# A hybrid decoder layer on one core: the high halves of two weight sets are kept in DRAM as well

## The chip, the cores and the metric

One core of one Trainium2 chip runs the kernel. The metric is the device time of one execution in microseconds; lower is better.

## The reference, cut to what is computed

One decoder layer is applied to 2048 prompt tokens and to 8 x 8 sample tokens, all in float32:

```python
h = rmsnorm(x, g_pre_mix)
z, q, k, v, glow, og = jnp.split(h @ w_in, SPLIT_IDX, axis=-1)          # 1024 -> 2064
pool_out = pool_mixer(z, ...)          # causal windows 2, 4, 8, 16, then a 128x128 map per group
gla_out = gla_mixer(q, k, v, gk, og)   # gated linear attention, 4 heads, exact per token
x = x + rmsnorm(concat(pool_out, gla_out) @ w_o, g_post_mix)
f = conv_ffn(rmsnorm(x, g_pre_ffn), ..., w_up, w_conv, b_conv, w_down)  # d_ff 2816, gated
x = x + rmsnorm(f, g_post_ffn)
x = x + (p @ w_ple) * jax.nn.sigmoid(x @ w_ple_gate)
```

## The kernel before

The tokens are cut into six tiles, `TILES`: tile 0 has 256 prompt tokens and the 64 sample tokens, tiles 1 to 4 have 384 prompt tokens each, tile 5 has 256. Features lie on the partitions and tokens in the columns. Every product with a large weight is made of three, since each operand is split into a high half, rounded to the matmul's float32r form, and a low half, the rest: high x high, high x low (weight), low (activation) x high. They are lines L1640, L1641 and L1642 in the function `product`.

The weights don't fit on the chip, so they stream past it once a tile. They are cut into *units* of 128 output columns, 512 KB each, in the fixed order that `plan` writes out: 16 units `in` (w_in), 8 units `o` (w_o), 44 units `up`, 24 parts `down`, 2 halves of `ple` and 8 units `gate`. In the text in5 means unit 5 of `in` of the tile at hand, gate3 unit 3 of `gate`. The ple halves and the gates of tile t are computed inside tile t+1: after in15 come the first ple half and gate0 to gate2, then o0 to o7, then the second ple half and gate3 to gate7, then up0. So tile 0's gates run in tile 1. Those of tile 5 stand at the end of the kernel.

A unit n uses slot n % 4 of the four slots. A slot has two buffers of 4 KB a partition: `stage` (the same bytes as `w_lo`) and `w_hi` (the same bytes as `w_whole`). There are two ways through a slot. In the plain way SP loads the unit into `stage`, ACT rounds it into `w_hi` (L730), and DVE subtracts in place, so that `w_lo` holds the low half (L1157). For `in` and `gate`, the low half that was made in the first pass is also stored to a DRAM tensor, `kept_lo` (L470). In all later passes SP loads the whole weights into `w_whole` (L483) and the low half into `w_lo` (L484), and ACT rounds in place; DVE has nothing to do.

The queues are in order and each engine's program follows the list of units. SP's is `load_unit(n)`: it first issues the stores of low halves that are due, up to unit n-3 (`keep_los(n - SLOTS + 1)`, each after a wait for `lo_made`), then waits until PE has ended unit n-4, waits for the landing of unit n-4's store if there was one, and then issues the load of unit n. All DMAs of the kernel are issued by SP on one queue. ACT, while PE is in unit n, first empties the bank of unit n-1 (`finish`), then makes the high half of unit n+2 (`make_hi(n + 2)`, which waits for its landing), and then does the rest of the work that is listed for this unit: decays, copies of v, squares, ple banks, copies of y. DVE makes the low half of unit n+1 (`make_lo(n + 1)`) ahead of its other work. PE waits for `hi_made` or `lo_made` at the start of a unit (`halves_ready`). The outputs go round over three PSUM banks, so PE also needs the bank of three outputs before.

Of the kernel before, what the change touches and what calls it, by code (L numbers as in the profile page):

```python
# [7 lines left out]
F32 = mybir.dt.float32  # L8
# [5 lines left out]
P = 128  # L14
D = 1024
KD = D // P
# [28 lines left out]
SLOTS = 4  # L45
# [17 lines left out]
def plan():  # L63

    units, outs, ticks = [], [], []

    def ple(t, s):
        units.append((t, "ple", s))
        for m in range(4 * s, 4 * s + 4):
            outs.append((t, "ple", m))  # L70
            ticks.append((t, "ple", m))

    def full(t, kind, m):
        for table in (units, outs, ticks):
            table.append((t, kind, m))

    for t in range(NT):
        for s in range(16):
            full(t, "in", s)
            if s >= 8 and s - 8 < chunks(t) + (TILES[t][2] > 0):  # L80
                outs.append((t, "v", s - 8))
        if t:
            ple(t - 1, 0)
            for m in range(EARLY_GATES):
                full(t - 1, "gate", m)
        for m in range(KD):
            full(t, "o", m)
        if t:
            ple(t - 1, 1)
            for m in range(EARLY_GATES, KD):  # L90
                full(t - 1, "gate", m)
        for m in range(2 * NF):
            full(t, "up", m)
        for m in range(3 * KD):
            units.append((t, "down", m))
            ticks.append((t, "down", m))
            if m % 3 == 0:
                outs.append((t, "down", m // 3))
    for s in range(2):
        ple(LAST, s)  # L100
    for m in range(KD):
        full(LAST, "gate", m)
    return units, outs, ticks


UNITS, OUTS, TICKS = plan()

KEPT_NO = {unit[1:]: j for j, unit in enumerate(unit for unit in UNITS if unit[0] == 0 and unit[1] in ("in", "gate"))}
KEEP_LO = [unit[0] == 0 and unit[1:] in KEPT_NO for unit in UNITS]
LOADS_LO = [unit[0] > 0 and unit[1:] in KEPT_NO for unit in UNITS]  # L110
LOS_MADE = list(itertools.accumulate(not loaded for loaded in LOADS_LO))
UNIT_NO = {name: n for n, name in enumerate(UNITS)}
OUT_NO = {name: n for n, name in enumerate(OUTS)}
# [33 lines left out]

def hybrid_layer(nc, x_prompt, x_sample, state_pool, state_gla, state_conv, p_prompt, p_sample, packed,
                 w_in_units, w_o_units, w_up_units, w_down_units, w_ple_units, w_gate_units,
                 kept_lo, y_prompt, y_sample, pool_prompt, gla_prompt, conv_prompt, pool_sample, gla_sample,  # L150
                 conv_sample):
    ctx = ExitStack()
    with ctx:
# [10 lines left out]
        def at(name, shape, offset, dtype=F32):  # L164
            return nc.alloc_sbuf_tensor_at(name, shape, dtype, offset=offset)
# [50 lines left out]
        w_lo = [at(f"w_lo{s}", [P, KD, P], slot_at[s], F32R) for s in range(SLOTS)]  # L216
        hi_at = [region(KD * P) for _ in range(SLOTS)]
        w_hi = [at(f"w_hi{s}", [P, KD, P], hi_at[s], F32R) for s in range(SLOTS)]
        w_whole = [at(f"w_whole{s}", [P, KD, P], hi_at[s]) for s in range(SLOTS)]
# [96 lines left out]
        def sem(name):  # L316
            return ctx.enter_context(nc.semaphore(name))
# [7 lines left out]
        landed = [sem(f"landed{s}") for s in range(SLOTS)]  # L325
        kept = [sem(f"kept{s}") for s in range(SLOTS)]
        hi_made, lo_made, ticks = sem("hi_made"), sem("lo_made"), sem("ticks")
# [72 lines left out]
        def exact(ap):  # L400
            return ap.bitcast(F32)
# [31 lines left out]
        def landing(n):  # L433

            return landed[n % SLOTS], 16 * sum(1 + LOADS_LO[k] for k in range(n % SLOTS, n + 1, SLOTS))

        def keeping(n):
            return kept[n % SLOTS], 16 * sum(KEEP_LO[k] for k in range(n % SLOTS, n + 1, SLOTS))

        def tick(name):  # L440
            return ticks, TICK_NO[name] + 1
# [1 line left out]
        def end_tick(unit):  # L443
            t, kind, m = unit
            return tick((t, "ple", 4 * m + 3)) if kind == "ple" else tick(unit)

        def parts_of(unit):
            return DOWN_PARTS[unit[2] % 3][1] if unit[1] == "down" else KD
# [3 lines left out]

        @block.sync
        def _(sp):
            keep_next = [0]

            def source(unit):
                t, kind, m = unit
                if kind == "down":
                    first_k, parts = DOWN_PARTS[m % 3]  # L460
                    return w_down_units[m // 3, :, first_k:first_k + parts, :]
                return {"in": w_in_units, "o": w_o_units, "up": w_up_units, "ple": w_ple_units,
                        "gate": w_gate_units}[kind][m]


            def keep_los(n):
                for k in range(keep_next[0], n + 1):
                    if KEEP_LO[k]:
                        sp.wait_ge(lo_made, LOS_MADE[k])
                        sp.dma_start(kept_lo[KEPT_NO[UNITS[k][1:]]], exact(w_lo[k % SLOTS][:, :, :])).then_inc(  # L470
                            kept[k % SLOTS], 16)
                keep_next[0] = n + 1

            def load_unit(n):
                unit = UNITS[n]
                if n >= SLOTS:
                    keep_los(n - SLOTS + 1)
                    sp.wait_ge(*end_tick(UNITS[n - SLOTS]))
                    if KEEP_LO[n - SLOTS]:
                        sp.wait_ge(*keeping(n - SLOTS))  # L480
                if LOADS_LO[n]:
                    s = n % SLOTS
                    sp.dma_start(w_whole[s][:, :, :], source(unit)).then_inc(landed[s], 16)  # L483
                    sp.dma_start(exact(w_lo[s][:, :, :]), kept_lo[KEPT_NO[unit[1:]]]).then_inc(landed[s], 16)  # L484
                    return
                dst = stage[n % SLOTS][:, 0:parts_of(unit), :]
                if unit[1] == "ple":
                    dst = dst.rearrange("p (k c) d -> p k (c d)", k=2)
                sp.dma_start(dst, source(unit)).then_inc(landed[n % SLOTS], 16)
# [36 lines left out]

            load_first_x()
            load_unit(0)
            sp.dma_start(const[:, 0:C_GK], packed[:, 0:C_GK]).then_inc(const_loaded, 16)
            load_unit(1)  # L530
            sp.dma_start(const[:, C_GK:C_ALL], packed[:, C_GK:C_ALL]).then_inc(tables_loaded, 16)
            load_unit(2)
            zs = state_pool[0].rearrange("b t (g c) -> (b t g) c", g=POOLG).rearrange("(q p) c -> p q c", p=120)
            sp.dma_start(z_state_tok[:, :, :], zs).then_inc(states_loaded, 16)
# [8 lines left out]
            for n in range(SLOTS, len(UNITS)):  # L543
                t, kind, m = UNITS[n]
# [170 lines left out]
        def _(act):  # L715
# [4 lines left out]
            def make_hi(n):  # L720
                for k in range(hi_next[0], min(n + 1, len(UNITS))):
                    one_hi(k)
                hi_next[0] = max(hi_next[0], n + 1)

            def one_hi(n):
                if n < len(UNITS):
                    s, parts = n % SLOTS, parts_of(UNITS[n])
                    whole = w_whole[s] if LOADS_LO[n] else stage[s]
                    act.wait_ge(*landing(n))
                    act.activation(w_hi[s][:, 0:parts, :], whole[:, 0:parts, :], ACT.Copy).then_inc(hi_made, 1)  # L730
# [408 lines left out]
        def _(dve):  # L1139
# [8 lines left out]
            def make_lo(n):  # L1148
                for k in range(lo_next[0], min(n + 1, len(UNITS))):
                    one_lo(k)  # L1150
                lo_next[0] = max(lo_next[0], n + 1)

            def one_lo(n):
                if n < len(UNITS) and not LOADS_LO[n]:
                    s, parts = n % SLOTS, parts_of(UNITS[n])
                    dve.wait_ge(hi_made, n + 1)
                    dve.tensor_tensor(w_lo[s][:, 0:parts, :], stage[s][:, 0:parts, :], exact(w_hi[s][:, 0:parts, :]),  # L1157
                                      ALU.subtract).then_inc(lo_made, 1)

# [463 lines left out]
        def _(pe):  # L1623
# [261 lines left out]
                y_turned.did(last, t, m)  # L1885

            def halves_ready(n):
                if LOADS_LO[n]:
                    pe.wait_ge(hi_made, n + 1)
                else:  # L1890
                    pe.wait_ge(lo_made, LOS_MADE[n])

# [250 lines left out]
```

## Time and profile before

| | |
|---|---|
| median of 3 runs | 2621.26 us (2618.65 to 2623.07) |
| the profiled execution | 2621.26 us, span 2619.6 us |
| PE busy | 2572.4 us (98%), mean granted clock 0.993 |
| DVE, ACT busy | 1578.4 us (60%), 1355.1 us (52%) |
| DMA | 415.95 MB, mean 159 GB/s; written to DRAM 22.89 MB |
| chain that ended last | PE 94%, DVE 2%, ACT 2%, DMA 1% |

The span is what the trace covers, from the first instruction to the last. In the rows further down a unit is a run of 24 products on PE. In SP's timeline a line is the issue of a DMA, not its transfer: how long a transfer takes is its time from issue to landing. A wait stands in square brackets behind the instruction that waited, with its length and what ended it.

### The profile page before, as it was taken

To read this page: it belongs to the slowest core of one execution; us is meant where nothing else is said; L and a number is where in the kernel's file an instruction comes from. 1 tells how busy PE (TensorE), PEld (TensorE's weight loads), DVE (VectorE), ACT (ScalarE), POOL (GpSimd) and SP (SyncE) were. 2 spreads that over 40 slices of the span, in tenths; PEclk is the share of its full clock that TensorE was granted. 3 is DMA by queue.
4 is the path that set the end of the run, shared out by engine and by line. 5 is a ranking of instruction groups with operands and counts; after the bars stand their busy time and mean duration, and the time that the engine had idled before them with its cause. 6 is when DMAs were issued, how large, how long until landed. Compare 5 with 4: busy or idle time off the path is not lost.

```text
span 2619.6 us, 41342 instructions
## 1 busy us (share of the span) xinstructions
PE 2572.4 (98%) x16538; PEld 2508.1 (96%) x16538; DVE 1578.4 (60%) x2525; ACT 1355.1 (52%) x2156; POOL 163.7 (6%) x492
## 2 busy tenths in 40 slices
PE   7989999999999999999999999999999999999998
PEld 6889999999999999999999999999999999999997
DVE  5668754566665455666545666554556654547864
ACT  4555554555444456544445654444565444566554
POOL 3200100100000010000001000000100000100000
PEclk9999999999999999999999999999999999999999
DMA  7435546454434644443464444345444434755565
GB/s 205 145 101 177 161 142 211 148 165 143 147 124 125 207 139 165 148 151 121 123 207 143 163 145 153 124 118 206 145 161 146 144 125 124 263 178 193 187 180 196
DMA packets 123107, 415.95 MB, mean 159 GB/s; under 512 B 12862, under 2 KB 21222, under 8 KB 122918
## 3 DMA queue, kind: packets, MB, share of 16 engines
q1 hardware_dynamic: 122918, 413.32, 48.2%
q8 instruction: 132, 2.16, 0.3%
q14 instruction: 57, 0.47, 0.1%
HBM read 390.38 MB, written 22.89 MB: 158 GB/s over the span
## 4 chain that ended last, share of the span: by engine, by line
PE 94%; DVE 2%; ACT 2%; DMA 1%; issue 1%; SPq 0%; DVEq 0%; ACTq 0%
PE G L1640 29%; PE G L1641 28%; PE G L1642 28%; PE X L1699 2%; PE X L1633 1%; PE X L1636 1%; DMA w_lo<-kept_lo 1%; PE X L1826 1%; PE X L1754 1%; PE X L1769 0%; ACT w_hi L730 0%; DVE w_lo L1157 0%; PE G L1633 0%; DVE A L1248 0%; PE X L1678 0%
## 5 line engine op out<-in xcount | busy, mean ns | idle before, releaser
L1640 PE MATMUL G<-h_hi,w_hi 128*128 128x384 f32 (+2 forms) x3264 | 1070.6, 328 | 16.9 <-DVE w_lo L1157 6.8
L1641 PE MATMUL G<-h_hi,w_lo 128*128 128x384 f32 (+2 forms) x3264 | 1052.3, 322 | 0.0
L1642 PE MATMUL G<-h_lo,w_hi 128*128 128x384 f32 (+2 forms) x3264 | 1052.3, 322 | 0.0
L730 ACT ACTIVATE w_hi<-stage 128x1024 fp32r<-128x1024 f32 (+1 forms) x492 | 510.6, 1038 | 397.2 <-DMA stage<-in_w_up_units_dram 236.0
L1157 DVE TENSOR_TENSOR w_lo<-stage,w_hi 128x1024 fp32r<-128x1024 f32 (+1 forms) x492 | 588.1, 1196 | 161.6 <-ACT w_hi L730 161.3
L1640 PEld LDWEIGHTS G<-h_hi,w_hi 128*128 128x128 f32 x3264 | 617.9, 189 | 23.4 <-issue 10.3
L1641 PEld LDWEIGHTS G<-h_hi,w_lo 128*128 128x128 f32 x3264 | 618.4, 189 | 1.7 <-issue 0.4
L1642 PEld LDWEIGHTS G<-h_lo,w_hi 128*128 128x128 f32 x3264 | 617.6, 189 | 0.0
L1640 PE MATMUL G<-y_hi,w_hi 128*128 128x384 f32 (+2 forms) x1056 | 346.3, 328 | 0.0
L1642 PE MATMUL G<-y_lo,w_hi 128*128 128x384 f32 (+2 forms) x1056 | 339.6, 322 | 0.0
L1641 PE MATMUL G<-y_hi,w_lo 128*128 128x384 f32 (+2 forms) x1056 | 339.5, 321 | 0.0
L1420 DVE SCALAR_TENSOR_TENSOR cg<-gx,const,cg 128x384 f32<-128x384 f32 (+1 forms) x264 | 151.5, 574 | 85.8 <-ACT cg L902 62.2
L1640 PEld LDWEIGHTS G<-y_hi,w_hi 128*128 128x128 f32 x1056 | 199.0, 188 | 4.0 <-issue 2.9
L1641 PEld LDWEIGHTS G<-y_hi,w_lo 128*128 128x128 f32 x1056 | 199.1, 189 | 1.1
L1642 PEld LDWEIGHTS G<-y_lo,w_hi 128*128 128x128 f32 x1056 | 198.9, 188 | 0.0
L1408 DVE TENSOR_TENSOR gx<-G,rms_up 128x384 f32<-128x384 f32 (+1 forms) x132 | 67.5, 511 | 197.8 <-PE G L1642 179.5
L730 ACT ACTIVATE w_hi<-w_whole 128x1024 fp32r<-128x1024 f32 x120 | 126.7, 1056 | 67.0 <-DMA w_lo<-kept_lo 66.4
L1165 DVE TENSOR_TENSOR total<-total,sq 128x384 f32<-128x384 f32 (+2 forms) x119 | 62.4, 524 | 157.2 <-ACT sq L743 156.9
L909 ACT ACTIVATE cg<-cg 128x384 f32<-128x384 f32 (+2 forms) x132 | 65.9, 500 | 173.7 <-DVE cg L1420 141.5
L1640 PE MATMUL G<-xg_hi,w_hi 128*128 128x384 f32 (+2 forms) x384 | 128.3, 334 | 3.8 <-DVE xg_lo L1459 2.3
L743 ACT ACTIVATE sq<-G 128x384 f32<-128x384 f32 (+2 forms) x84 | 39.1, 465 | 167.7 <-PE G L1642 167.7
L1642 PE MATMUL G<-xg_lo,w_hi 128*128 128x384 f32 (+2 forms) x384 | 123.4, 321 | 0.0
(234 smaller groups left out, 2673.9 us busy)
## 6 DMA issues: line engine op xcount, KB each, us to landing
stage<-in_w_up_units_dram SPq DMA_DIRECT2D x264, 512.0 KB, 3.5
w_lo<-kept_lo SPq DMA_DIRECT2D x120, 512.0 KB, 4.5
stage<-in_w_down_units_dram SPq DMA_DIRECT2D x96, 448.0 KB, 3.3
w_whole<-in_w_in_units_dram SPq DMA_DIRECT2D x80, 512.0 KB, 3.5
stage<-in_w_o_units_dram SPq DMA_DIRECT2D x48, 512.0 KB, 3.5
stage<-in_w_down_units_dram SPq DMA_DIRECT2D x48, 512.0 KB, 3.5
w_whole<-in_w_gate_units_dram SPq DMA_DIRECT2D x40, 512.0 KB, 3.6
kept_lo<-w_lo SPq DMA_DIRECT2D x24, 512.0 KB, 5.2
```

Of the source, the lines that this page charges most:

```text
L730: act.activation(w_hi[s][:, 0:parts, :], whole[:, 0:parts, :], ACT.Copy).then_inc(hi_made, 1)
L743: squared.did(act.activation(out[:, 0:width(t)], src[:, 0:width(t)], ACT.Square), t, m)
L909: gelu_made.did(act.activation(c[:, 0:w], c[:, 0:w], ACT.Gelu_apprx_tanh), t, f)
L1157: dve.tensor_tensor(w_lo[s][:, 0:parts, :], stage[s][:, 0:parts, :], exact(w_hi[s][:, 0:parts, :]), ALU.subtract).then_inc(lo_made, 1)
L1165: added.did(dve.tensor_tensor(start[:, 0:w], start[:, 0:w], ring[:, m % 2, 0:w], ALU.add), t, m - 1)
L1408: last = dve.tensor_tensor(x[:, 2:2 + np_], G[b][:, 0:np_], rms_up[:, 0:np_], ALU.mult)
L1420: last = dve.scalar_tensor_tensor(c[:, 0:np_], x[:, k:k + np_], tap, c[:, 0:np_], ALU.mult, ALU.add)
L1633: return pe.transpose(out, in_, ident[0:n, 0:n])
L1640: pe.matmul(ps[:, 0:w], l_hi, r_hi[:, 0:w], start=start, stop=False)
L1641: pe.matmul(ps[:, 0:w], l_lo, r_hi[:, 0:w], start=False, stop=False)
L1642: return pe.matmul(ps[:, 0:w], l_hi, r_lo[:, 0:w], start=False, stop=stop)
L1699: last = pe.matmul(X[first + b][:, col:col + 64], opnd[n % 2][r, d, cols(c)], queries[n % 2][r, d, 64 * c:64 * c + 64], start=True, stop=True)
```

## The change

The high halves of `in` and `gate` are kept in DRAM too. A new tensor `kept_hi` takes them. For `gate` both halves are stored in the first pass (tile 0's gates). For `in` the low half is stored in the first pass, as before, and the high half in the second (tile 1), in which it is still made by ACT from the whole weights. After that (`in` from tile 2 on, `gate` from tile 1's gates on) SP loads the high half straight into `w_hi`, ACT makes nothing for these units, and PE waits for the landing itself. The stores are issued at another place: `keep_halves(n - SLOTS)` is called directly ahead of the load of unit n, for the unit whose slot that load will overwrite, where the stores up to unit n-3 were issued before. SP's wait for the landing of the stores stays where it was, behind the wait for PE's end of unit n-4, and now also covers the high half's.

```diff
+KEEP_HI = [unit[1:] in KEPT_NO and unit[0] == (1 if unit[1] == "in" else 0) for unit in UNITS]
 LOADS_LO = [unit[0] > 0 and unit[1:] in KEPT_NO for unit in UNITS]
+LOADS_HI = [lo and not hi for lo, hi in zip(LOADS_LO, KEEP_HI)]
+HIS_MADE = list(itertools.accumulate(not loaded for loaded in LOADS_HI))
...
         def keeping(n):
-            return kept[n % SLOTS], 16 * sum(KEEP_LO[k] for k in range(n % SLOTS, n + 1, SLOTS))
+            return kept[n % SLOTS], 16 * sum(KEEP_LO[k] + KEEP_HI[k] for k in range(n % SLOTS, n + 1, SLOTS))
...
-            def keep_los(n):
-                for k in range(keep_next[0], n + 1):
-                    if KEEP_LO[k]:
-                        sp.wait_ge(lo_made, LOS_MADE[k])
-                        sp.dma_start(kept_lo[KEPT_NO[UNITS[k][1:]]], exact(w_lo[k % SLOTS][:, :, :])).then_inc(
-                            kept[k % SLOTS], 16)
-                keep_next[0] = n + 1
+            def keep_halves(n):
+                s, name = n % SLOTS, UNITS[n][1:]
+                if KEEP_HI[n]:
+                    sp.wait_ge(hi_made, HIS_MADE[n])
+                    sp.dma_start(kept_hi[KEPT_NO[name]], exact(w_hi[s][:, :, :])).then_inc(kept[s], 16)
+                if KEEP_LO[n]:
+                    sp.wait_ge(lo_made, LOS_MADE[n])
+                    sp.dma_start(kept_lo[KEPT_NO[name]], exact(w_lo[s][:, :, :])).then_inc(kept[s], 16)
 
             def load_unit(n):
                 unit = UNITS[n]
                 if n >= SLOTS:
-                    keep_los(n - SLOTS + 1)
+                    keep_halves(n - SLOTS)
                     sp.wait_ge(*end_tick(UNITS[n - SLOTS]))
-                    if KEEP_LO[n - SLOTS]:
+                    if KEEP_LO[n - SLOTS] or KEEP_HI[n - SLOTS]:
                         sp.wait_ge(*keeping(n - SLOTS))
                 if LOADS_LO[n]:
-                    s = n % SLOTS
-                    sp.dma_start(w_whole[s][:, :, :], source(unit)).then_inc(landed[s], 16)
-                    sp.dma_start(exact(w_lo[s][:, :, :]), kept_lo[KEPT_NO[unit[1:]]]).then_inc(landed[s], 16)
+                    s, j = n % SLOTS, KEPT_NO[unit[1:]]
+                    if LOADS_HI[n]:
+                        sp.dma_start(exact(w_hi[s][:, :, :]), kept_hi[j]).then_inc(landed[s], 16)
+                    else:
+                        sp.dma_start(w_whole[s][:, :, :], source(unit)).then_inc(landed[s], 16)
+                    sp.dma_start(exact(w_lo[s][:, :, :]), kept_lo[j]).then_inc(landed[s], 16)
                     return
...
             def one_hi(n):
-                if n < len(UNITS):
+                if n < len(UNITS) and not LOADS_HI[n]:
...
             def halves_ready(n):
-                if LOADS_LO[n]:
-                    pe.wait_ge(hi_made, n + 1)
+                if LOADS_HI[n]:
+                    pe.wait_ge(*landing(n))
+                elif LOADS_LO[n]:
+                    pe.wait_ge(hi_made, HIS_MADE[n])
                 else:
                     pe.wait_ge(lo_made, LOS_MADE[n])
```

## Rows read from the trace of the kernel before

**Rows 1.** The page, parts 1 and 4: busy time and last chain, by engine.

```profile
PE 2572.4 (98%) x16538; PEld 2508.1 (96%) x16538; DVE 1578.4 (60%) x2525; ACT 1355.1 (52%) x2156; POOL 163.7 (6%) x492
...
PE 94%; DVE 2%; ACT 2%; DMA 1%; issue 1%; SPq 0%; DVEq 0%; ACTq 0%
```

**Rows 2.** The page, part 5: the splitting of the weights on DVE and ACT.

```profile
L1157 DVE TENSOR_TENSOR w_lo<-stage,w_hi 128x1024 fp32r<-128x1024 f32 (+1 forms) x492 | 588.1, 1196 | 161.6 <-ACT w_hi L730 161.3
...
L730 ACT ACTIVATE w_hi<-w_whole 128x1024 fp32r<-128x1024 f32 x120 | 126.7, 1056 | 67.0 <-DMA w_lo<-kept_lo 66.4
```

**Rows 3.** The page, part 6: DMA issues, median us from issue to landing.

```profile
w_lo<-kept_lo SPq DMA_DIRECT2D x120, 512.0 KB, 4.5
...
w_whole<-in_w_in_units_dram SPq DMA_DIRECT2D x80, 512.0 KB, 3.5
...
kept_lo<-w_lo SPq DMA_DIRECT2D x24, 512.0 KB, 5.2
```

**Rows 4.** The DMA queue's timeline in tile 0 (start, length, what).

```profile
41.81 0.38 SPq L489 DMA_DIRECT2D stage<-in_w_in_units_dram  x1
...
83.26 0.33 SPq L489 DMA_DIRECT2D stage<-in_w_in_units_dram  x1
83.64 0.43 SPq L470 DMA_DIRECT2D kept_lo<-w_lo  x1
...
103.66 5.58 SPq L489 DMA_DIRECT2D stage<-in_w_o_units_dram  x2
```

**Rows 5.** The DMA queue's timeline in tile 1: the loads of in3 and in13.

```profile
413.74 0.33 SPq L483 DMA_DIRECT2D w_whole<-in_w_in_units_dram  x1
...
468.16 0.33 SPq L483 DMA_DIRECT2D w_whole<-in_w_in_units_dram  x1
```

**Rows 6.** DMA issues at 77.9, 572.5, 1130.5 and 1130.9, 1131.8: us to landing.

```profile
kept_lo<-w_lo SPq DMA_DIRECT2D x1, 512.0 KB, 5.4
...
kept_lo<-w_lo SPq DMA_DIRECT2D x1, 512.0 KB, 2.9
...
stage<-in_w_up_units_dram SPq DMA_DIRECT2D x1, 512.0 KB, 4.0
x_tok<-in_x_prompt_dram SPq DMA_DIRECT2D x1, 512.0 KB, 4.8
...
x_tok<-in_x_prompt_dram SPq DMA_DIRECT2D x1, 512.0 KB, 6.7
```

**Rows 7.** ACT's timeline in tile 1, at the first half of ple.

```profile
504.44 1.05 ACT L730 ACTIVATE w_hi<-stage 128x1024 fp32r<-128x1024 f32 x1
```

**Rows 8.** PE's timeline there: the start of ple, and a wait.

```profile
505.50 0.39 PE L1640 MATMUL G<-p_hi,w_hi 128*128 128x320 f32 x1
...
509.36 0.42 PE L1640 MATMUL G<-p_hi,w_hi 128*128 128x320 f32 x1 [0.98 <-ACT ple L949]
```

**Rows 9.** The DMA queue's timeline in tile 1: the load of gate6.

```profile
564.72 0.33 SPq L489 DMA_DIRECT2D stage<-in_w_gate_units_dram  x1
```

**Rows 10.** PE's timeline in tile 1: the first product of up3.

```profile
602.17 0.33 PE L1640 MATMUL G<-h_hi,w_hi 128*128 128x384 f32 x1
```

**Rows 11.** Windows on PE: busy us by engine, granted clock, DMA share, GB/s.

```profile
160.00:166.00 6.00, 4.22 (x14) 3.86 (x15) 5.86 (x14) 3.61 (x9) 0.00 (x0) 0.59 0.00 0
...
2575.00:2581.00 6.00, 4.21 (x22) 3.83 (x21) 0.51 (x2) 3.73 (x8) 0.00 (x0) 0.72 0.69 226
```

**Rows 12.** The waits of PE in tiles 2 to 4 (total us, times, longest).

```profile
PE G L1640 <- ACT ple L949: 3.7, 4, 2.1
```

**Rows 13.** ACT's and PE's timelines in the last 45 us.

```profile
2575.89 1.06 ACT L730 ACTIVATE w_hi<-w_whole 128x1024 fp32r<-128x1024 f32 x1 [1.87 <-DMA w_lo<-kept_lo]
...
2590.26 1.04 ACT L730 ACTIVATE w_hi<-w_whole 128x1024 fp32r<-128x1024 f32 x1
...
2577.27 0.39 PE L1640 MATMUL G<-p_hi,w_hi 128*128 128x256 f32 x1 [1.79 <-ACT ple_last L949]
...
2604.52 0.44 PE L1633 MATMUL X<-ident,sig 128*128 128x128 f32 x2 [1.00 <-ACT y_tok L965]
```

More of the change, by code:

```diff
@@ L149, in hybrid_layer @@
                  w_in_units, w_o_units, w_up_units, w_down_units, w_ple_units, w_gate_units,
-                 kept_lo, y_prompt, y_sample, pool_prompt, gla_prompt, conv_prompt, pool_sample, gla_sample,
+                 kept_hi, kept_lo, y_prompt, y_sample, pool_prompt, gla_prompt, conv_prompt, pool_sample, gla_sample,
                  conv_sample):
@@ L454, in _ @@
         def _(sp):
-            keep_next = [0]
             def source(unit):
@@ L1155, in one_lo @@
                     s, parts = n % SLOTS, parts_of(UNITS[n])
-                    dve.wait_ge(hi_made, n + 1)
+                    dve.wait_ge(hi_made, HIS_MADE[n])
                     dve.tensor_tensor(w_lo[s][:, 0:parts, :], stage[s][:, 0:parts, :], exact(w_hi[s][:, 0:parts, :]),
@@ L2136 @@
         args.append(nc.dram_tensor(f"in_{name}_dram", a.shape, F32, kind="ExternalInput").ap())
-    args.append(nc.dram_tensor("kept_lo", (len(KEPT_NO), P, KD, P), F32, kind="Internal").ap())
+    for name in ("kept_hi", "kept_lo"):
+        args.append(nc.dram_tensor(name, (len(KEPT_NO), P, KD, P), F32, kind="Internal").ap())
     for n, shape in enumerate(_OUTS):
```

## The prediction

> **What bounds the kernel now.** I read the page first. PE is busy for 98% of the span, and 94% of the chain that ended last is PE's [rows 1], so the kernel can gain at most the 47 us in which PE idles, and anything that makes PE wait is paid in full. The splitting of weights costs ACT 1.06 us and DVE 1.2 us a unit [rows 2], but both engines have room: ACT is busy 52%, DVE 60% [rows 1]. The question is therefore which PE waits end on the work that is removed, and which new ones end on the work that is added. So I read next the waits of PE, then the timeline of the DMA queue, which shows when each unit's slot is refilled, then the landings, and last ACT's timeline where it holds PE up.
>
> **What the DMA queue does today.** SP issues the load of unit n when PE has ended unit n-4, so the issue times are also PE's pace. The load has three units of time before PE needs it. A store of a low half is issued one unit before the slot is wanted again: it goes out at 83.64, right behind the load of 83.26 [rows 4], and the wait for it comes only one load later. That is why 24 stores of 5.2 us each [rows 3] cost nothing.
>
> **Part 1: the stores move onto the queue's own path.** In the new code the store of unit n-4 is issued immediately ahead of load n, and SP then waits for it to land before load n goes out. It thus sits behind load n-1, which went out a moment before, and queued behind SP's wait are load n and all that follow. One load and the landing of one store must now pass in each step. I call this the round trip.
>
> In tile 0 (in1 to in15) a step is one load and one store. The store is issued 0.38 us after the load [rows 4] and lands 5.4 us later [rows 6]: P0 = 5.8 us. PE's pace there is (103.66 - 41.81)/12 = 5.15 us a unit [rows 4]. SP loses 0.65 us a unit, some 8 to 9 us by the last one. A unit's slack is three units less landing and splits, 15.5 - 7 = 8.5 us. So this uses up the slack and costs PE about 1 us; the bounds are 0 and 5 (5.8 against 6.2 us a step).
>
> **Part 2: 24 stores more.** The high halves of tile 1's in units, and of tile 0's gates (computed in tile 1), are stored too.
>
> *Tile 1, in units.* A step is now two loads and one store. The second load is issued some 0.4 us after the first (the first's issue takes 0.33 [rows 5]) and lands 4.5 us later [rows 3]: both are there after 4.9 us. No row shows three. Below: four loads in a row were issued from 1130.5 to 1131.8; the first lands at 1134.5, the second at 1135.7, the fourth at 1138.5 [rows 6], so one more transfer of 512 KB adds 1.2 to 1.4 us at the queue's full rate: with 1.25, 6.15 us. Above: a store behind a load adds 5.8 - 3.5 = 2.3 us [rows 3, 6]: 7.2 us. I take the middle, P1 = 6.7. PE's pace is (505.5 - 413.74)/16 = 5.7 us a unit [rows 5, 8], less than even the low end. The step repeats 13 times from the load of in3 at 413.74 to the load of the first ple half, then twice with one load and one store (P0) to the load of gate1: 413.74 + 13 x 6.7 + 2 x 5.8 = 512.4. It needs 4.0 us to land (the first of the four loads) [rows 6] and 1.05 us of ACT [rows 7]: 517.5. ACT does this work at PE's start of ple, ahead of everything that follows there, and PE's start is 505.5 [rows 8]. So PE is 12.0 us late by then. With P1 = 6.15 it is 4.9, with 7.2 it is 18.5. Part of it shows earlier, in the in units: ACT waits in order for the landing of the unit two ahead, and the decays, the copies of v and so the PSUM banks stand behind that wait; in10 starts at 468.16 today [rows 5], and in11's load would go out at 413.74 + 8 x 6.7 = 467.3. These are the same 12 us, not more.
>
> *Tile 1, gates 3 to 7.* A step is one load and two stores: 5.8 + 1.25 = 7.1 us, or at most 5.8 + 2.3 = 8.1. There are five, from the load of gate6 at 564.72 [rows 9] to that of up3: 600.2. Landing 3.5 [rows 3], 1.06 and 1.2 for the halves [rows 2] make 606.0, and PE starts up3 at 602.17 [rows 10]: 3.8 us late. I take 5, since the subtraction also stands in order among DVE's other work. With 8.1 it is 9. Gates 0 to 2 have the same step three times ahead of o units, and the 12 us of lateness covers them.
>
> *The clock.* Where PE had idled 3.7 us the granted clock in the next 6 us was 0.59, and 0.72 around a wait of 1.8 us [rows 11]; the level falls from 2.4 GHz to 1.2 for a part of them. New waits of this kind cost some 2 us more (0 to 4), as the queue catches up in the meantime.
>
> The Trainium skill (DMA: Bandwidth & Descriptors, on the two cost components of a DMA) puts the fixed cost of a DMA mostly on the confirmation of the write and calls a target in HBM the heaviest. The trace has a lone store at 2.9 us and a lone load at 3.5 [rows 3, 6], which disagrees, but 0.9 us more for a store than for a load behind a load, which agrees; by the rule alone P1 would be the upper bound. The same page fits 2.0 us plus bytes over 436 GB/s; an estimate from it for 1.5 MB is 5.6 us, less than PE's pace, and the new waits would vanish.
>
> **Part 3: what ACT is spared.** From tile 2 on (in units) and for the gates of tiles 1 to 5, 104 splits of 1.06 us vanish. Most lie beside PE's work and give nothing. Two places count. At the first ple half, ACT splits gate1 [rows 7] before it empties the ple banks, for which PE waits 0.98 us [rows 8]; tiles 2 to 4 show the same, 3.7 us in four waits [rows 12]. Four tiles (2 to 5) at 0.95: 4 us. At the end of the kernel, ACT waits 1.87 us for a gate's landing and splits it, and PE waits 1.79 us for the bank behind it; another split of 1.04 stands ahead of the first sigmoid, and a turn of y waits 1.00 us behind a third [rows 13]; with half a microsecond of slow clock [rows 11] that is 4 us. Together 8 us; 4 if the chain through DVE takes over at the end, 9 at most. That the high half now comes from the stored copy changes no bytes: two loads of 512 KB as before.
>
> **Sum.** +1 +12 +5 +2 -8 = +12 us on the profiled execution's 2621.26 us (span 2619.6 and 1.7 around it), which is also the median: 2633. Lower ends: 0 + 4.9 + 3.8 + 0 - 8 = +1, 2622. Upper ends: 5 + 18.5 + 9 + 4 - 4 = +32, 2653.
>
> **The rivals.**
> *The queue is quick enough* (other side). If two loads and a store pass in 5.7 us or less, because stores run beside loads on the 16 DMA engines, SP never falls behind in tile 1, and the gates' two stores stay inside the slack. Then the gain stands alone: 2621.3 - 8 = 2613. For it: the DMA engines are at 0.69 in a window with pairs of loads, not full [rows 11]. Against: a store behind a load is the slowest landing of all [rows 6]. It decides at a step of 5.7 us. The fit of the Trainium skill quoted above, 5.6, would put it here. Chance 0.15.
> *The costs cancel.* A step near 6.2 us, tile 0 hidden: +9 - 8, so 2621 to 2623. For it: the rate of four loads in a row [rows 6]. Chance 0.2.
> *The waits feed each other.* ACT waits in order, so a late landing also holds decays, evacuations and DVE's subtractions; in tile 0 PE falls behind as well, and the clock drops more often. Tile 0 gives 10 instead of 1, the clock 8 instead of 2, steps of 7.2: about +45, 2665. Against: three units of slack. Chance 0.1.
> *No change*, since ACT and DVE are off the path anyway: this needs the stores to be hidden as well and the end's waits not to shrink; it lies inside the second.
>
> **How the numbers follow.** My forecast of 2633 has 0.55 (its own range 2623 to 2653), the others 0.15, 0.2, 0.1. A difference under 0.2% (5.2 us) is about what a measurement cannot tell from none. Faster than 2616: 0.16; within: 0.2 and a little of the forecast's low end, 0.22; slower than 2626.5: 0.62. The range 2616 to 2653 leaves out the first and the last rival, with the tails.
>
> **What would show it.** Right: SP's waits for kept stores become the largest waits of its queue in tile 1; its loads of in4 to in15 go out about 6.7 us apart; PE idles between 440 and 530 and again at 590 to 615, some 17 us in all; ple waits from tile 2 on are gone and the end after 2570 is about 4 us shorter. Wrong: a spacing under 5.8 us, or PE's new waits in tile 0, would move the sum to the first or third rival.

## The result, and the profile after

The changed kernel takes 2646.05 us (median of 4 runs, 2643.8 to 2649.27) against 2619.95 for the kernel before: ratio 1.010, interval 1.0083 to 1.0118. It is slower by 26 us. The forecast had the sign, but with 12 us less than half of the size.

The page of the changed kernel: busy time by engine, the DMA totals, the chain that ended last, and three of its DMA issues.

```profile
PE 2579.2 (98%) x16538; PEld 2515.1 (95%) x16538; DVE 1576.4 (60%) x2525; ACT 1253.9 (47%) x2052; POOL 160.2 (6%) x492
...
HBM read 390.38 MB, written 35.48 MB: 161 GB/s over the span
...
PE 91%; DMA 4%; DVE 2%; ACT 1%; issue 1%; SPq 0%; POOL 0%; DVEq 0%; POOLq 0%; ACTq 0%
...
w_lo<-kept_lo SPq DMA_DIRECT2D x120, 512.0 KB, 4.6
w_hi<-kept_hi SPq DMA_DIRECT2D x104, 512.0 KB, 3.7
...
kept_lo<-w_lo SPq DMA_DIRECT2D x24, 512.0 KB, 5.4
kept_hi<-w_hi SPq DMA_DIRECT2D x24, 512.0 KB, 6.2
```

ACT has lost the 104 splits (101 us less than in [rows 1]), and as many bytes are read as before. The new thing is DMA in the chain that ended last: 4% against 1% [rows 1]. What the DMA queue waited for (total us, times, longest) names it, in the kernel before and then in the changed one:

```profile
SPq L480 <- DMA kept_lo<-w_lo: 13.1, 8, 5.7
```

```profile
SPq L483 <- DMA kept_lo<-w_lo: 124.1, 24, 6.5
SPq L483 <- DMA kept_hi<-w_hi: 94.2, 16, 7.6
```

SP waits 218 us for stores to land, where it waited 13. Its timeline in tile 1, from the load of in3 on, answers to [rows 5]:

```profile
417.37 0.33 SPq L489 DMA_DIRECT2D w_whole<-in_w_in_units_dram  x1
417.74 0.43 SPq L490 DMA_DIRECT2D w_lo<-kept_lo  x1
418.22 0.43 SPq L472 DMA_DIRECT2D kept_hi<-w_hi  x1
425.18 0.33 SPq L489 DMA_DIRECT2D w_whole<-in_w_in_units_dram  x1
...
432.54 0.33 SPq L489 DMA_DIRECT2D w_whole<-in_w_in_units_dram  x1
...
439.77 0.33 SPq L489 DMA_DIRECT2D w_whole<-in_w_in_units_dram  x1
```

Two loads, a store, and then nothing until the store has landed. The median spacing from in3 to in15 is 7.3 us, where PE needs 5.7. Three of the steps took 7.8 to 8.9 us, so that the mean of the thirteen steps to the load of the first ple half is 7.5. The chain that ended last, in tile 1 of the changed kernel between 440 and 540 us (start, length, what; the first pieces of a row of twelve of this kind, and the end):

```profile
440.62 6.39 DMA kept_hi<-w_hi
447.92 6.34 DMA kept_hi<-w_hi
455.18 6.92 DMA kept_hi<-w_hi
...
515.33 5.00 DMA kept_hi<-w_hi
520.78 5.27 DMA kept_hi<-w_hi
526.11 4.44 DMA stage<-in_w_gate_units_dram
533.64 1.48 ACT out_sq L862
```

For this stretch 76% of the chain is the landing of one store after another. It ends as foreseen: in the load of gate1, ACT's work at the first ple half, and PE.

Where PE's lateness arises is seen by setting the same product of both traces side by side. The table gives PE's start in microseconds.

| first product of | before | changed | late by |
|---|---|---|---|
| in0, tile 0 | 22.4 | 23.5 | 1.1 |
| in0, tile 1 | 413.5 | 417.2 | 3.6 |
| gate0 (in tile 1) | 513.9 | 541.6 | 27.6 |
| up4, tile 1 | 606.3 | 642.3 | 35.9 |
| first ple half at the end | 2573.2 | 2601.4 | 28.3 |
| span | 2619.6 | 2642.8 | 23.2 |

So the start is 1.1 us later, tile 0 costs 2.6 us, tile 1's in units and ple half 24.0, tile 1's last gates 8.3, and all that follows gives back 12.7.

### The profile page after: what moved, and what is told of

The parts are those of the page before. It is cut to its first block, busy times and chain, and to the rows that moved or that the text cites. A ratio compares the mean times of both kernels' runs of the same rounds, so it can differ in the third digit from the quotient of the medians.

```text
span 2642.8 us, 41278 instructions
## 1 busy us (share of the span) xinstructions
PE 2579.2 (98%) x16538; PEld 2515.1 (95%) x16538; DVE 1576.4 (60%) x2525; ACT 1253.9 (47%) x2052; POOL 160.2 (6%) x492
## 4 chain that ended last, share of the span: by engine, by line
PE 91%; DMA 4%; DVE 2%; ACT 1%; issue 1%; SPq 0%; POOL 0%; DVEq 0%; POOLq 0%; ACTq 0%
PE G L1646 28%; PE G L1647 28%; PE G L1648 28%; DMA kept_hi<-w_hi 3%; PE X L1705 2%; PE X L1639 1%; PE X L1642 1%; DMA kept_lo<-w_lo 1%; PE X L1832 1%; PE X L1775 1%; PE X L1760 0%; DVE w_lo L1163 0%; DMA stage<-in_w_up_units_dram 0%; DMA stage<-in_w_in_units_dram 0%; PE X L1781 0%
## 5 line engine op out<-in xcount | busy, mean ns | idle before, releaser
L1647 PE MATMUL G<-xg_hi,w_lo 128*128 128x384 f32 (+2 forms) x384 | 124.1, 323 | 0.0
```

Of the source, the lines that this page charges most:

```text
L1647: pe.matmul(ps[:, 0:w], l_lo, r_hi[:, 0:w], start=False, stop=False)
```

## The experiments

Each kernel is compared with the kernel before in runs on the same chip. All are built from the changed kernel unless the text says otherwise. Their table stands after the last of them.

**The stores back at their old place.** The stores go out where the kernel before issues them; everything else is as changed.

```diff
-                    keep_halves(n - SLOTS)
+                    while keep_next[0] <= n - SLOTS + 1:
+                        keep_halves(keep_next[0])
+                        keep_next[0] += 1
```

> The changed kernel, but each unit's stores are issued where the kernel before issues them, up to unit n-3 ahead of load n, so that a store is waited for only one load later; the same 48 stores, the same bytes. Theory A (the loss is the round trip of a load and a store's landing that now stands on the queue's own path): the steps of 7.3 us in tile 1 and 5.7 us in tile 0 vanish, the spacing of the loads of tile 1 follows PE again (about 5.7 us), and what is left is the gain, which the trace of the changed kernel shows as 12.7 us from tile 2 on: 2607 us, 2603 to 2612. Theory B (the 12.6 MB of stores more slow the loads themselves): most of the 24 us of tile 1's in units and the 8 us of its last gates stay: 2630 us or more.

Measured: 2609.07 us against 2619.85, ratio 0.9958 (0.9946 to 0.9971). All 48 stores and their bytes are still there, and tile 1's cost is gone. Theory B falls. The landings in tile 1 between 415 and 490 us show how much slower the transfers may become without cost:

```profile
kept_hi<-w_hi SPq DMA_DIRECT2D x14, 512.0 KB, 8.3
w_whole<-in_w_in_units_dram SPq DMA_DIRECT2D x13, 512.0 KB, 5.2
w_lo<-kept_lo SPq DMA_DIRECT2D x13, 512.0 KB, 7.4
```

The changed kernel has its transfers of tile 1 land sooner (between 425 and 510 us):

```profile
w_whole<-in_w_in_units_dram SPq DMA_DIRECT2D x12, 512.0 KB, 4.1
w_lo<-kept_lo SPq DMA_DIRECT2D x12, 512.0 KB, 5.6
kept_hi<-w_hi SPq DMA_DIRECT2D x12, 512.0 KB, 6.4
```

It is the slower kernel by 37 us all the same. What counts is not how long a transfer takes but what is held back until it has landed.

**The late place alone.** The kernel before, with `keep_los(n - SLOTS)` for `keep_los(n - SLOTS + 1)`.

> The kernel before with one argument changed: the store of a low half is issued ahead of the load that overwrites its slot, one unit later than before; no high half is kept. Theory A: tile 0's steps are 5.7 to 5.8 us as in the changed kernel, where PE was 3.9 us late at the start of tile 0's up1 (5.3 from its best point); the last gates of tile 1 have steps of 5.8 us and need 0 to 1 us: plus 4 to 6 us, 2625 us. Theory B: the number of bytes is that of the kernel before, so 2620 us.

Measured: 2625.49 against 2619.85, ratio 1.0024 (1.0014 to 1.0033). The place costs time without a byte more, 5.6 us, as theory A had it. The profiled execution is only 2.5 us longer than that of before; in it tile 0 costs 2.8 us and tile 1's last gates 0.2.

**High halves of in units alone.** `KEEP_HI` and `LOADS_HI` are true for `in` only.

> The changed kernel, but high halves are kept for the in units alone; the gates are split on ACT each time, as before. Theory A: tile 0 costs 4 us, tile 1's in units and first ple half 24, its last gates 0 to 1; the gain is nearly gone, since the ple waits and the end of the kernel hang on the splits of gates (12.7 us less some 11): plus 26, 2646 us, as slow as the changed kernel with two thirds of its stores. Theory B: two thirds of the stores' 32 us of tile 1, 21, without the gain: 2641.

Measured: 2652.27, ratio 1.0123 (1.0109 to 1.0136), 6 us above the 2646 of theory A and further still from theory B. Tile 1's in units cost 23.1 us, its last gates 0.1. The kernel is 6 us slower than the changed one, which has more stores: the in units bring the loss and none of the gain. This run's first product starts 4.0 us later than in the trace of before. The start is shifted by -0.1 to 4.2 us in these traces, by 3.2 us also where the stores are at their old place, so it is not taken for an effect of the edits.

**The gain alone.** The first experiment without the stores of high halves; the high buffer is filled from the kept low halves.

```diff
-                if KEEP_HI[n]:
-                    sp.wait_ge(hi_made, HIS_MADE[n])
-                    sp.dma_start(kept_hi[KEPT_NO[name]], exact(w_hi[s][:, :, :])).then_inc(kept[s], 16)
...
-                        sp.dma_start(exact(w_hi[s][:, :, :]), kept_hi[j]).then_inc(landed[s], 16)
+                        sp.dma_start(exact(w_hi[s][:, :, :]), kept_lo[j]).then_inc(landed[s], 16)
```

> Leaves out: no high half is stored, and from tile 2 on (gates: tile 1) the buffer of the high half is loaded with the kept low half instead, so the values of these products are not those of the reference; bytes loaded, waits and splits left out are those of the changed kernel, and the low halves' stores stand where they did before. Both theories: no loss, only the gain of the splits that ACT is spared, 12.7 us: 2607 us. My prediction had 8: 2612.

Measured: 2608.09 against 2619.85: 11.8 us, close to the 12.7 expected. With the first experiment's 10.8 it says that 24 stores more cost 1 us, if anything, when they go out early; the intervals of the two overlap.

**The step made smaller, larger, and of another kind.** Three kernels change only what stands late in tile 1's in units: half the store, the store twice, and a load in the store's stead. The first and the third leave out what they don't store: from tile 2 on their in units load the kept low half into the high buffer, so these products are not the reference's.

```diff
+                    parts = KD if UNITS[n][1] == "gate" else KD // 2
-                    sp.dma_start(kept_hi[KEPT_NO[name]], exact(w_hi[s][:, :, :])).then_inc(kept[s], 16)
+                    sp.dma_start(kept_hi[KEPT_NO[name], :, 0:parts, :], exact(w_hi[s][:, 0:parts, :])).then_inc(kept[s], 16)
...
-                        sp.dma_start(exact(w_hi[s][:, :, :]), kept_hi[j]).then_inc(landed[s], 16)
+                        sp.dma_start(exact(w_hi[s][:, :, :]), (kept_lo if unit[1] == "in" else kept_hi)[j]).then_inc(landed[s], 16)
```

> The changed kernel, but in tile 1 only half of each in unit's high half (256 KB) is stored, at the same place; leaves out the other half, and from tile 2 on the in units load the kept low half into the high buffer, so their products are not the reference's. Measured step in tile 1 with the whole store: 7.3 us. If a store behind two loads costs by its bytes at the queue's full rate (0.6 us for 256 KB) and the rest is fixed, the step is 6.7 us, tile 1's in units and ple cost 15 instead of 24 us, and the time is 2637 us. If the whole 2.3 us of a store are bytes, the step is 6.15 and the time 2628 us. If it is all fixed: 7.3 us and 2646.

Measured: 2628.59, ratio 1.0031 (1.0021 to 1.0041), step 6.2 us: the second of the three cases. In the next edit `kept_hi` has twice the size and `keeping` counts the second store too.

```diff
                     sp.dma_start(kept_hi[KEPT_NO[name]], exact(w_hi[s][:, :, :])).then_inc(kept[s], 16)
+                    if UNITS[n][1] == "in":
+                        sp.dma_start(kept_hi[KEPT_NO[name] + len(KEPT_NO)], exact(w_hi[s][:, :, :])).then_inc(kept[s], 16)
```

> The changed kernel, but in tile 1 each in unit's high half is stored twice, the second time to DRAM that nobody reads. Theory A: the step grows by 1.3 us (full rate) to 8.6 us, PE's lateness by 13 such steps, 17 us, since all slack is used up already: 2663 us. With 2.3 us a store: 9.6 us and 2676. A theory in which the loss is not the step on the queue's path gives no more than 3 us: 2649.

Measured: 2675.28, ratio 1.0209 (1.0195 to 1.0223), step 9.2 us, near the case of 2.3 us a store (2676). In the next edit `spare` is a buffer that nobody uses; the load of the high buffer is as in the first of the three.

```diff
-                    sp.dma_start(kept_hi[KEPT_NO[name]], exact(w_hi[s][:, :, :])).then_inc(kept[s], 16)
+                    if UNITS[n][1] == "in":
+                        sp.dma_start(spare[:, :, :], w_in_units[UNITS[n][2]]).then_inc(kept[s], 16)
+                    else:
+                        sp.dma_start(kept_hi[KEPT_NO[name]], exact(w_hi[s][:, :, :])).then_inc(kept[s], 16)
```

> The changed kernel, but in tile 1 the late store of each in unit's high half is replaced by a load of the same 512 KB from DRAM into an unused buffer, issued and waited for at the same place; leaves out the stores, and from tile 2 on the in units load the kept low half into the high buffer, so their products are not the reference's. If only the third transfer counts, the step stays 7.3 us and the time 2646. If it is the store's direction that costs the 0.9 us more (three loads in a row took 6.4 us from the first issue), the step is 6.4, tile 1's in units and ple cost 8 to 11 us instead of 24, and the time is 2632 us.

Measured: 2636.66, ratio 1.0063 (1.0048 to 1.0078), step 6.6 us, between its two cases. Median landings in the three, in tile 1's in units; each fence shows the late transfer of one kernel, first the half store, then the double one (both of its stores), then the load, with the two loads ahead of it:

```profile
kept_hi<-w_hi SPq DMA_DIRECT2D x15, 256.0 KB, 5.2
```

```profile
kept_hi<-w_hi SPq DMA_DIRECT2D x30, 512.0 KB, 6.9
```

```profile
spare<-in_w_in_units_dram SPq DMA_DIRECT2D x14, 512.0 KB, 5.7
w_whole<-in_w_in_units_dram SPq DMA_DIRECT2D x12, 512.0 KB, 3.4
w_lo<-kept_lo SPq DMA_DIRECT2D x12, 512.0 KB, 4.5
```

What follows: half a store less takes 1.1 us off the step, so by its bytes a store of 512 KB costs 2.2 to 2.3 us there. The step without any late transfer would be 4.9 [rows 3], so of the store's 2.4 us hardly anything seems to be a fixed part; the half store also has rows of half the length, which no run separates. A second store adds 1.9. A load at the same place adds 1.7, 0.7 us less than a store. And a store slows the loads that were issued before it: they land after 4.1 and 5.6 us in the changed kernel, after 3.4 and 4.5 with a load behind them. The cost in tile 1 follows the step: 5.2 us at 6.2, 13.2 at 6.6, 24.0 at 7.3, 50.6 at 9.2. From the changed kernel to the double store that is 26.6/1.9 = 14 us for each microsecond of step, from the half store 17, for thirteen steps.

**Gates alone, early.** The first experiment with `KEEP_HI` and `LOADS_HI` true for `gate` only.

> High halves kept for the gates alone (8 stores of high halves instead of 24), stores issued early as in the kernel before. Theory: the splits of in units lie beside PE's work and give nothing, those of the gates give all: 2608 us, the same as with both kept and stored early (2609). Rival: the in units' splits give their share (64 of 104): 2614.

Measured: 2609.18, ratio 0.9960 (0.9948 to 0.9973): the same as with both kept. The 64 splits of in units are worth nothing that the runs can tell; the 40 of gates are the gain.

**Gates alone, late.** The changed kernel with `KEEP_HI` and `LOADS_HI` true for `gate` only.

> The changed kernel with high halves kept for the gates alone, stores late as in the change. By the steps of the earlier runs: tile 0 costs 2.7 us (late lows), tile 1's in units nothing (their step is two loads and no store), its last gates 8, and the gain is 11: plus 0, 2620 us (2617 to 2623), that is, two thirds of the high halves' stores gone and all of the loss but 8 us of it. If the loss hung on all 48 stores alike, a third of the high ones would leave some 11 of the 24 us: 2631.

Measured: 2623.22 against 2620.92, ratio 1.0010 (1.0001 to 1.0020), within the expected 2617 to 2623 but for 0.2 us. Tile 1's in units cost nothing, its last gates 7.2.

**The late store on another queue.** The in units' high halves are stored from ACT's queue when PE starts the unit. SP waits for them where it did.

```diff
-                if KEEP_HI[n]:
+                if KEEP_HI[n] and name[0] == "gate":
                     sp.wait_ge(hi_made, HIS_MADE[n])
...
+                if KEEP_HI[n] and kind == "in":
+                    act.wait_ge(hi_made, HIS_MADE[n])
+                    act.dma_start(kept_hi[KEPT_NO[(kind, m)]], exact(w_hi[n % SLOTS][:, :, :])).then_inc(kept[n % SLOTS], 16)
                 make_hi(n + 2)
```

> The changed kernel, but the in units' high halves are stored from ACT's queue when PE starts the unit, as late as SP does it, and SP only waits for them where it did; same 48 stores, same bytes. If the loss is the order on SP's own queue (a store issued behind a late load, and the next load behind that store's landing, so that the lateness is never made good), the spacing follows PE again (5.9 us), tile 1's in units cost 0 to 4 us, and the time is 2646 - 24 + 2 = 2624 us (2619 to 2630). If it is only that a store issued in PE's unit n-4 has to land before load n, wherever it is issued from, the step stays at 7 us and the time over 2640.

Measured: 2623.62 against 2620.92, ratio 1.0012 (1.0003 to 1.0021). Tile 1's in units cost 0.0 us, its last gates 9.6. SP's waits, and the landings between 425 and 510 us:

```profile
SPq L483 <- DMA kept_hi<-w_hi: 64.9, 16, 7.1
```

```profile
kept_hi<-w_hi ACTq DMA_DIRECT2D x14, 512.0 KB, 5.2
w_lo<-kept_lo SPq DMA_DIRECT2D x12, 512.0 KB, 6.0
```

SP still waits for these stores, and the loads land late, but the store's issue hangs on PE and not on the load before, so that a late load makes the next store no later. The lateness does not add up: three steps between in5 and in10 took 7.9 to 8.0 us, the ones behind them 1.5 to 4.6. One thing more is different: the store lands after 5.2 us, against 6.4 in the changed kernel, and this run doesn't tell how much of the cure is that. The second queue makes the loads no faster: the low half lands after 6.0 us, against 5.6. The Trainium skill (DMA: Bandwidth & Descriptors, on issuing engines that are not separate DMA queues) says the queues share the same 16 engines; the later loads agree.

All runs: the step is the median spacing of the loads from in3 to in15 of tile 1. The costs are differences of PE's position between the products named in the table above, less those of the trace before. "After up4" is the change from up4 to the end of the span.

| kernel | median us | step | tile 0 | in and ple, tile 1 | last gates | after up4 |
|---|---|---|---|---|---|---|
| changed | 2646.05 | 7.3 | 2.6 | 24.0 | 8.3 | -12.7 |
| stores at the old place | 2609.07 | 5.9 | -1.7 | 0.0 | 0.0 | -12.5 |
| late place alone | 2625.49 | 5.9 | 2.8 | 0.0 | 0.2 | -1.4 |
| in alone, late | 2652.27 | 7.4 | 2.8 | 23.1 | 0.1 | -0.5 |
| gain alone | 2608.09 | 5.9 | -1.5 | 0.0 | 0.0 | -11.5 |
| half store | 2628.59 | 6.2 | 2.4 | 5.2 | 7.4 | -12.7 |
| double store | 2675.28 | 9.2 | 5.3 | 50.6 | 8.6 | -11.6 |
| load for store | 2636.66 | 6.6 | 2.4 | 13.2 | 7.3 | -12.7 |
| gates alone, early | 2609.18 | 5.9 | -0.1 | 0.0 | 0.0 | -10.4 |
| gates alone, late | 2623.22 | 5.9 | 4.0 | 0.0 | 7.2 | -8.3 |
| in stores on ACT's queue | 2623.62 | 6.1 | 4.7 | 0.0 | 9.6 | -11.5 |

## Why the prediction was wrong in size

**The mechanism was right.** The forecast's first part, that the store's round trip comes to stand on the queue's own path, is shown: the old place removes the loss with all bytes in place, the late place alone brings a loss without them, and the chain of waits runs through the stores. The rival that the queue is quick enough fell with the spacing of 7.3 us against PE's 5.7. The rival that the costs cancel fell with it.

**The step P1 of tile 1 is the term that failed.** The prediction took the middle, 6.7 us, of 6.15 (a further transfer at the queue's full rate) and 7.2 (a store behind a load). Measured: 7.3 in the median and 7.5 in the mean of the thirteen steps, above both. The upper row was the better one to go by, since it was a store; the lower was worked out from loads. With a load at that place the step is 6.6 us, so the lower row was too low for a load as well. The forecast's own formula with what the trace shows, 97.3 us for the thirteen steps, 11.5 for the two behind them, 4.4 for the landing of gate1 and 1.06 for its split, and with all times counted from the 3.6 us by which tile 1 starts late, gives 413.74 + 97.3 + 11.5 + 5.5 - 505.5 = 22.5 us, where it gave 12.0 before the run. The thirteen steps are 10.2 us of this difference. The term is thus past its own upper end of 18.5; that the time stays under 2653 all the same is because tile 0 and the last gates stayed well below theirs and the gain was larger.

PE's wait for the ple bank, [rows 8] at 509.36, agrees: it now ends at 535.50, 26.1 us later, and 3.6 of these were there at in0. The same formula gives 4.4, 11.5, 23.1 and 48.7 us for the half store, the load, the in units alone and the double store, which measured 5.2, 13.2, 23.1 and 50.6.

**The clock was the second, and smaller.** The windows of both stretches (from 9.5 us ahead of in0 to gate0, and on to up4), in the changed kernel and then in the kernel before; the columns are length, then busy us of PE, weight loads, DVE, ACT and POOL, granted clock, DMA share, GB/s:

```profile
407.70:541.74 134.04, 116.83 (x753) 109.62 (x751) 55.56 (x92) 54.15 (x92) 12.02 (x15) 0.92 0.67 211
541.74:642.44 100.70, 92.77 (x539) 89.94 (x537) 64.55 (x99) 59.28 (x106) 1.26 (x5) 0.95 0.54 184
```

```profile
404.00:513.91 109.91, 108.18 (x753) 102.43 (x752) 55.36 (x91) 53.78 (x92) 12.04 (x15) 1.00 0.54 183
513.91:606.33 92.42, 88.63 (x538) 85.73 (x537) 64.42 (x99) 59.96 (x107) 1.26 (x5) 1.00 0.47 154
```

The same products took PE 8.6 us more in the first stretch and 4.1 in the second, at a granted clock of 0.92 and 0.95 instead of 1.00: parts of both ran at the 1.2 GHz level (0.50 to 0.51 granted around 443 to 450, 484 to 491, 508 to 511, 535 to 539, 607 to 610 and 634 to 641 us), each around or right behind a wait of PE. The wait alone doesn't settle it: one of 1.5 us ahead of 607 is in the trace of before too, where the clock stayed. Most of this slow work cost nothing, because the chain through tile 1's in units runs over the stores and not over PE. The kernel with in units alone shows it: 17 us of PE's work in its in units were at that level too, and its 23.1 us are the formula's. What is left for the clock is 1.5 us of tile 1's 24.0, between the ple bank and gate0 (535 to 539). The prediction had 2 us (0 to 4) for all of it; with the last gates' 2.8 below it is 4.3.

**Tile 1's last gates** cost 8.3 us, and the forecast was 5 (3.8 to 9). Their step is 7.0 us, the 7.1 of the forecast. PE starts up3 5.5 us later than it would from gate0's lateness (635.33 against 602.17 [rows 10]): the steps, the landing and the halves give 3.3, and the other 2.2 are the subtraction for up3, which DVE began at 634.06, when ACT's split had ended at 631.81. It stood behind DVE's work on `cg`, in the order that the forecast named. The last 2.8 us come after that, at the 1.2 GHz level around 634 to 641. PE's idle time grew by 15.5 us in the first stretch and 4.1 in the second, 19.6 in all, where the forecast had some 17.

**Where PE stands still.** The forecast said that part of the lateness shows earlier, through ACT's order. It is most of it: at in13 PE is 20.8 us later than at in0. The largest wait of PE in tile 1, and ACT just before it:

```profile
484.46 1.06 ACT L736 ACTIVATE w_hi<-w_whole 128x1024 fp32r<-128x1024 f32 x1 [6.14 <-DMA w_lo<-kept_lo]
...
486.64 0.57 ACT L832 ACTIVATE v_tok<-G 128x512 f32<-128x512 f32 x1
```

```profile
487.36 0.66 PE L1646 MATMUL G<-h_hi,w_hi 128*128 128x384 f32 x1 [6.42 <-ACT v_tok L832]
```

ACT waits 6.14 us for the landing of a unit that PE needs only two units later, and behind this wait stands the copy of v whose PSUM bank PE needs now. A slot's slack of three units was never to be had in full, because ACT looks at the landing two units ahead. This is read from the program's order and the trace; no run changed that order. There are four waits of 2.7 to 6.4 us in the stretch, each of which ends, at once or over DVE, on ACT's work behind such a landing, and it is around waits like these that the clock fell.

**Tile 0** cost 2.6 us and the forecast was 1 (0 to 5); its step is 5.7, as expected. The same cost appears with the late place alone (2.8), and it is 2.4 to 5.3 in all kernels with late stores. The kernels with the stores at the old place show -1.7 to -0.1 there, so these costs are sure to about 1.5 us. The third rival (10 us there, 8 of clock) did not come. Its terms, with a gain of 8, also make some 34 to 38 us and not the 45 that it names.

**The gain** was sized 8 us (4 to 9) and is 8.3 to 12.7 in the traces of all kernels that load the gates' high halves, 11.8 in the runs that have it alone. The ple waits are gone, as the waits of PE between 880 and 2350 us show, where the ple line of [rows 12] no longer stands:

```profile
PE X L1705 <- DVE A L1254: 2.3, 3, 0.8
```

The forecast read the four waits of [rows 12] as those of tiles 2 to 4. They are one in each of tiles 2 to 5: three of 0.53 us and tile 5's of 2.10, at 2309.9 us. Tiles 2 to 4 give 0.8 us each, of the 0.95 forecast. Tile 5 gives 5.1: 3.7 at its first ple half, where besides the wait a dip of the granted clock to the 1.2 GHz level is missing that the trace of before has behind it at 2311 to 2315 us, and most of the rest at the second half. In "gates alone, late", which has the 8.3, there is such a wait and a dip in tile 5 (2302 to 2306 us) as well. The end gives 5 instead of 4. That the gates' splits and not the in units' are the gain is shown by the two kernels with gates alone, and by the one with in units alone, where only 0.5 us comes back.

**The sum** with what the profiled executions show, in the forecast's terms: +1.1 (start) + 2.6 (tile 0) + 22.5 (tile 1) + 5.5 (last gates) + 4.3 (clock) - 12.7 = +23.3 us; the spans differ by 23.2. The forecast's terms were 1 + 12 + 5 + 2 - 8. The medians are 26 us apart, 3 us more than these two executions; single executions of the changed kernel differ by up to 5.5 us.

One thing stays open: why a store behind loads takes 0.7 us longer than a load there. Part of it is that the two loads ahead land later when it is a store. The Trainium skill (DMA: Bandwidth & Descriptors, on the two cost components of a DMA) would blame the confirmation of a write to HBM. That half the bytes took away half of the store's cost speaks against a fixed part of this size. The same section of the Trainium skill states its fit of 2.0 us plus bytes over 436 GB/s for one DMA issued from GpSimd, where all of these are issued by SP; taken over, it gives the estimate of 5.6 us for the three transfers on which the first rival leaned. The step measured 6.6 us for three loads and 7.3 with a store, so the fit can't be used for a step of this kind.

## What to carry to other kernels

A wait on a queue that issues loads is priced by what is queued behind it: here the same store cost nothing when it was issued one unit ahead of its wait, and 24 us in tile 1 when it was issued directly before. If the round trip of one step is longer than the consumer's pace, the lateness adds up with every step once the slack is used; so measure the step with transfers of the same direction, and take its mean, since 6.7 us in place of 7.5 was multiplied by thirteen. Keep the halves of the gates alone and store them early: 2609 us, 0.4% faster than before, with a third of the new stores.

## What the runs showed of the hardware

Transfers in flight together slow one another and still deliver more: with three a unit issued early, loads land after 5.2 and 7.4 us instead of 3.5 and 4.4 and a store after 8.3, at 294 GB/s instead of 191 and at no cost to PE. A store of 512 KB behind two loads adds 2.4 us to the 4.9 in which the two have landed [rows 3], and a load 1.7; the store also makes the loads ahead of it land 0.7 and 1.1 us later. And waits of PE slow its work around them: with 15.5 us more idle time the same products took 8.6 us longer, at a granted clock of 0.92. How much of that is paid hangs on whether PE is on the path there: 1.5 us in tile 1's in units and ple half, 2.8 in its last gates.
